# Modulation sums moved from the gate/up layer to the down layer, and a third buffer for raw gate/up weights

## The reference, cut to what matters

```python
def swiglu(u, w_gate_up, w_down):            # D_FF = 2816 = 22 x 128
    gate, up = jnp.split(u @ w_gate_up, 2, axis=-1)
    return (jax.nn.silu(gate) * up) @ w_down
...
    c_act = jax.nn.silu(c)                   # c: one row of 1024
    for layer in range(DEPTH_2):             # 2 layers, after the feed-forward
        mod = c_act @ ada_w[layer] + ada_b[layer]      # 1024 -> 3072
        shift, scale, gate = jnp.split(mod, 3, axis=-1)
        h = rms_norm(x, norm_w[layer]) * (1.0 + scale[:, None, :]) + shift[:, None, :]
```

## Time and profile before

| what | us |
|---|---|
| median of 3 runs | 2910.16 |
| lowest and highest of them | 2908.41, 2910.83 |
| the profiled execution | 2912.97 |
| its span | 2911.1 |
| PE busy | 2809.6 (97%) |
| DVE busy | 1868.6 (64%) |
| ACT busy | 1298.0 (45%) |
| POOL busy | 720.9 (25%) |

### The profile page before, as it was taken

The page is one execution under the profiler, slowest core; times in us unless marked ns, Lnnn a source line. Parts: engine busy times, 40 slices in busy tenths (PEclk is TensorE's granted clock), DMA queues, the critical chain, the costliest instruction groups (busy, mean ns, idle before and its releaser), DMA issues.

```text
span 2911.1 us, 37370 instructions
## 1 busy us (share of the span) xinstructions
PE 2809.6 (97%) x14198; PEld 2344.0 (81%) x14198; DVE 1868.6 (64%) x2554; ACT 1298.0 (45%) x2086; POOL 720.9 (25%) x921
## 2 busy tenths in 40 slices
PE   8999999999999999999999999899999899999998
PEld 7877787778888778888888778788888778888986
DVE  7564475764456788887334745789878745318974
ACT  5321347432454322223112345678767624417851
POOL 0000003300002666663000011466545200004520
PEclk9999999999999999999999999999999999999999
DMA  4111333232311344446311323100001331131032
GB/s 150 54 44 56 124 107 135 93 116 87 102 59 55 106 151 156 144 148 227 105 47 42 111 73 91 40 1 16 8 15 37 109 109 40 48 94 65 18 117 73
DMA packets 201521, 245.46 MB, mean 84 GB/s; under 512 B 11776, under 2 KB 152320, under 8 KB 199808
## 3 DMA queue, kind: packets, MB, share of 16 engines
q1 hardware_dynamic: 184320, 186.37, 20.0%
q0 software_dynamic: 9104, 28.32, 3.2%
q10 hardware_dynamic: 7920, 28.38, 2.9%
HBM read 192.11 MB, written 46.20 MB: 82 GB/s over the span
## 4 chain that ended last, share of the span: by engine, by line
PE 83%; DVE 8%; issue 2%; ACT 2%; POOL 2%; DMA 1%; ACTq 0%; DVEq 0%; SPq 0%; POOLq 0%
PE P L349 47%; PE P L286 5%; PE P L289 5%; PE P L291 5%; PE P L290 5%; PE P L2728 4%; PE P L318 2%; PE P L2742 2%; PE P L2741 1%; PE P L1116 1%; PE P L1590 1%; PE P L3334 1%; DVE U L1839 1%; POOL T L2990 1%; PE P L3328 1%
## 5 line engine op out<-in xcount | busy, mean ns | idle before, releaser
L273 DVE TENSOR_TENSOR wl<-wf,wh 128x1024 fp32r<-128x1024 f32 (+3 forms) x163 | 192.8, 1183 | 658.9 <-ACT wh L265 658.4
L265 ACT ACTIVATE wh<-wf 128x1024 fp32r<-128x1024 f32 (+3 forms) x163 | 167.0, 1025 | 766.7 <-PE P L349 705.5
L349 PE MATMUL P<-XH,wh 128*128 128x512 f32 (+1 forms) x1232 | 385.1, 394 | 6.2 <-DVE TMP L1393 2.5
L349 PE MATMUL P<-XL,wh 128*128 128x512 f32 (+1 forms) x1232 | 381.3, 391 | 0.0
L349 PE MATMUL P<-XH,wl 128*128 128x512 f32 (+1 forms) x1232 | 381.0, 391 | 0.0
L2990 POOL TENSOR_TENSOR T<-T,WST 128x512 f32<-128x512 f32 x256 | 260.9, 1040 | 219.8 <-DVE WST L2960 197.0
L349 PEld LDWEIGHTS P<-XH,wh 128*128 128x128 f32 (+1 forms) x1232 | 229.4, 187 | 61.4 <-issue 12.0
L349 PEld LDWEIGHTS P<-XH,wl 128*128 128x128 f32 (+1 forms) x1232 | 229.8, 187 | 51.1
L349 PEld LDWEIGHTS P<-XL,wh 128*128 128x128 f32 (+1 forms) x1232 | 229.8, 187 | 51.0
L289 PE MATMUL P<-FO,U 128*128 128x512 f32 x616 | 242.6, 394 | 8.3 <-DVE T L2103 6.6
L290 PE MATMUL P<-FO,U 128*128 128x512 f32 x616 | 240.1, 390 | 0.0
(11 more groups left out here) (478 smaller groups left out, 6257.1 us busy)
## 6 DMA issues: line engine op xcount, KB each, us to landing
AW<-ada_t POOLq DMA_DIRECT2D x96, 256.0 KB, 3.5
wf<-gu_units SPq DMA_DIRECT2D x88, 256.0 KB, 3.0
H<-scratch_h SPq DMA_DIRECT2D x32, 512.0 KB, 6.3
wf<-w_in SPq DMA_DIRECT2D x28, 512.0 KB, 3.8
scratch_h<-H SPq DMA_DIRECT2D x24, 512.0 KB, 5.7
scratch_g<-T ACTq DMA_DIRECT2D x22, 512.0 KB, 3.0
scratch_f<-T ACTq DMA_DIRECT2D x22, 512.0 KB, 3.2
wf<-odd_w_in SPq DMA_DIRECT2D x20, 512.0 KB, 4.0
```

The costliest lines, as they stand in the source:

```text
L265: e.activation(self.sb["wh"][i % 2][:, 0:m], self.sb["wf"][i % 2][:, 0:m], ACT.Copy).then_inc(*self.s.w_hi.up(i))
L273: e.tensor_tensor(l, f, h.bitcast(F32), ALU.subtract).then_inc(*self.s.w_lo.up(i))
L349: ins = e.matmul(self.P[slot][0:m, t:t1], w, x[:, k, t:t1], start=first and k == 0, stop=last and k == kb - 1)
```

## The change

All 48 columns of the modulation leave the gate/up layer. They are now loaded as whole rows of 1024 numbers (48 loads of 512 KB) and summed by one instruction each, three behind each of the first 16 tiles of the down layer, on DVE behind the low part of the block. The places for them are one new place in region A and two of the scratch tiles (`T[3]`, `T[1]`), which are free once the last pair is done. The load of `c` and its silu also move to the end of the gate/up layer; POOL's loads start there. The space of the old halves becomes a third raw place (`UR`), so the load of unit `u` waits for the low part of unit `u-3`, and unit 2's for the end of the layer before (`wo`, tile 7), whose input lies there until then.

```diff
     def raw(self, u):
-        return self.sb["wf"][(self.no["wo", 6] + u) % 2]
+        return (self.sb["wf"][self.no["wo", 7] % 2], self.sb["wf"][self.no["wo", 6] % 2], self.sb["UR"])[u % 3]
...
     def sp_unit(self, e, u):
-        e.wait_ge(*self.s.w_lo.to(("u", u - 2) if u > 1 else self.no["wo", 6 + u]))
-        e.dma_start(self.raw(u)[:, 0:512], self.dr["gu_units"][u]).then_inc(*self.s.u[u % 2].up(u))
+        if u == 2:
+            e.wait_ge(*self.s.mm.to(("wo", 7)))
+        else:
+            e.wait_ge(*self.s.w_lo.to(("u", u - 3) if u > 2 else self.no["wo", 7 - u]))
+        e.dma_start(self.raw(u)[:, 0:512], self.dr["gu_units"][u]).then_inc(*self.s.u[u % 3].up(u))
...
-    def dve_ada(self, e, h):
...
+    def pool_ada(self, e, n):
+        f = 128 * (n % 24)
+        if n > 2:
+            e.wait_ge(*self.s.dve.to(("ada", n - 3)))
+        e.dma_start(self.sb["AW"][n % 3], self.dr["ada_t"][n // 24][f:f + 128, :]).then_inc(*self.s.a[n % 3].up(n))
+
+    def dve_ada(self, e, n):
+        x, a = self.sb["AW"][n % 3], VECS["ada_b_2"][0] + n
+        e.wait_ge(*self.s.a[n % 3].to(n))
+        if n == 0:
+            e.wait_ge(*self.s.act.to("silu c"))
+        e.tensor_tensor_reduce(x, x, self.sb["AA"][:, :], 1.0, self.sb["vecs"][:, a:a + 1], ALU.mult, ALU.add,
+                               self.sb["MOD"][:, n:n + 1]).then_inc(*self.s.dve.up(("ada", n)))
+        if n % 8 == 7:
+            self.dve_ada_gain(e, n // 8)
...  sp_ffn
-        e.wait_ge(*s.w_lo.to(("u", UNITS - 2)))
+        e.wait_ge(*s.w_lo.to(("u", UNITS - 3)))
...
-            if b == 7:
-                e.wait_ge(*s.dve.to(("ada", 95)))
...  pool_ffn
-        for u in range(4):
+        for u in range(UNITS):
             self.pool_unit(e, u)
-        e.wait_ge(*self.s.mm.to(("wo", 7)))
+        e.wait_ge(*self.s.mm.to(self.unit_done(UNITS - 1)))
         e.dma_start(self.sb["AA"][:, :], self.dr["c_row"].partition_broadcast(128)).then_inc(*self.s.cr.up("in"))
         self.pool_ada(e, 0)
...
+        e.wait_ge(*self.s.dve.to(("ff", PAIRS - 1)))
+        for n in range(1, 48):
+            self.pool_ada(e, n)
...  act_ffn, behind the store of the last pair
+        e.wait_ge(*s.cr.to("in"))
+        e.activation(self.sb["AA"][:, :], self.sb["AA"][:, :], ACT.Silu).then_inc(*s.act.up("silu c"))
...  dve_ffn
-            for h in range(96):
-                if self.ada_unit(h) == u:
-                    self.dve_ada(e, h)
...  behind a tile of groups 0 and 1
                 if j < count:
                     self.dve_ffn_block(e, GROUPS[n + 1][0] + j)
+                for i in range(3):
+                    self.dve_ada(e, 24 * n + 3 * j + i)
```

More of the change, by code:

```diff
@@ L83 @@
             "act", "dve", "pool")
-    DMAS = ("w0", "w1", "vecs", "consts", "me", "m0", "m1", "dt", "a0", "a1", "ax", "xr", "rt", *(f"q{u}{n}" for u in range(2) for n in range(2)), "cr", "u0", "u1", "fs", "b0", "b1", "r0", "r1", "r2", "r3", "r4", "out",
+    DMAS = ("w0", "w1", "vecs", "consts", "me", "m0", "m1", "dt", "a0", "a1", "ax", "xr", "rt", *(f"q{u}{n}" for u in range(2) for n in range(2)), "cr", "u0", "u1", "u2", "a2", "fs", "b0", "b1", "r0", "r1", "r2", "r3", "r4", "out",
             *(f"f{n}{j}" for n in range(2) for j in range(8)), *(f"h{j}" for j in range(8)), *(f"g{j}" for j in range(8)), *(f"gl{j}" for j in range(8)))
@@ L97, in __init__ @@
         self.m = [m["m0"], m["m1"]]
-        self.a, self.ax, self.xr, self.rt = [m["a0"], m["a1"]], m["ax"], m["xr"], m["rt"]
+        self.a, self.ax, self.xr, self.rt = [m["a0"], m["a1"], m["a2"]], m["ax"], m["xr"], m["rt"]
         self.q, self.b, self.out = [[m[f"q{u}{n}"] for n in range(2)] for u in range(2)], [m["b0"], m["b1"]], m["out"]
         self.h = [m[f"h{j}"] for j in range(8)]
-        self.cr, self.fs, self.u = m["cr"], m["fs"], [m["u0"], m["u1"]]
+        self.cr, self.fs, self.u = m["cr"], m["fs"], [m["u0"], m["u1"], m["u2"]]
         self.f = [[m[f"f{n}{j}"] for j in range(8)] for n in range(2)]
@@ L1817, in pool_unit @@
         count = self.s.pool
-        e.wait_ge(*self.s.u[u % 2].to(u))
+        e.wait_ge(*self.s.u[u % 3].to(u))
         e.tensor_tensor(s1, a21, a22, ALU.add).then_inc(*count.up(("s1", u)))
@@ L1840, in dve_unit @@
                             ALU.subtract).then_inc(*self.s.w_lo.up(("u", u)))
[L1844 to L1854, removed]
-    def dve_ada(self, e, h):
[L1857 to L1861, removed]
-            e.wait_ge(*self.s.act.to("silu c"))
[L1863 to L1868, removed]
+    def pool_ada(self, e, n):
[7 more added lines that the diff above has]
+        if n == 0:
+            e.wait_ge(*self.s.act.to("silu c"))
+        e.tensor_tensor_reduce(x, x, self.sb["AA"][:, :], 1.0, self.sb["vecs"][:, a:a + 1], ALU.mult, ALU.add,
+                               self.sb["MOD"][:, n:n + 1]).then_inc(*self.s.dve.up(("ada", n)))
+        if n % 8 == 7:
+            self.dve_ada_gain(e, n // 8)
     def dve_ada_gain(self, e, i):
@@ L1875, in dve_ada_gain @@
         if part == 1:
-            e.wait_ge(*self.s.dve.to(("ada", 16 * i + 15)))
+            e.wait_ge(*self.s.dve.to(("ada", 8 * i + 7)))
             e.scalar_tensor_tensor(out=MOD, in0=MOD, scalar=1.0, in1=vecs[:, gain[0] + 8 * layer:gain[0] + 8 * layer + 8],
@@ L1954, in pool_ffn @@
     def pool_ffn(self, e):
-        for u in range(4):
+        for u in range(UNITS):
             self.pool_unit(e, u)
-        e.wait_ge(*self.s.mm.to(("wo", 7)))
+        e.wait_ge(*self.s.mm.to(self.unit_done(UNITS - 1)))
         e.dma_start(self.sb["AA"][:, :], self.dr["c_row"].partition_broadcast(128)).then_inc(*self.s.cr.up("in"))
         self.pool_ada(e, 0)
[L1960 to L1963, removed]
-            for h in range(96):
-                if self.ada_unit(h) + 3 == u:
-                    self.pool_ada(e, h + 2)
+        e.wait_ge(*self.s.dve.to(("ff", PAIRS - 1)))
+        for n in range(1, 48):
+            self.pool_ada(e, n)
     def pe_ffn(self, e):
@@ L2062, in act_ffn @@
                 e.activation(T[0][:, 0:512], self.gu_bank(m, 0), ACT.Copy).then_inc(*s.act.up(("p1", m)))
-            if u == 9:
-                e.wait_ge(*s.cr.to("in"))
-                e.activation(self.sb["AA"][:, :], self.sb["AA"][:, :], ACT.Silu).then_inc(*s.act.up("silu c"))
         for b in range(3, 7):
@@ L3718, in places @@
     sb["FX"] = put("FX", "X", 0, [128, 8, 2, S], F32R)
-    sb["AW"] = [put(f"AW{i}", "X", 28 * K + 2 * K * i, [128, 512], F32)[:, :] for i in range(2)]
-    sb["AA"] = put("AA", "X", 60 * K, [128, 1024], F32)
+    sb["UR"] = put("UR", "X", 28 * K, [128, 1024], F32)
+    sb["AW"] = [put("AW0", "A", 60 * K, [128, 1024], F32)[:, :], sb["T"][3], sb["T"][1]]
+    sb["AA"] = put("AA", "A", 56 * K, [128, 1024], F32)
     sb["ACC2"] = put("ACC2", "X", 60 * K, [128, 1024], F32)
```

## The result

The changed kernel takes 2917.19 us (median of 19 runs) against 2910.83 us of the kernel before (19 runs on the same chips): a ratio of 1.0019, 95% interval [1.0012, 1.0026]. I had forecast 2904.1 us, 0.2% faster; by the ratio it is about 5.5 us slower. A second set of runs of both kernels gave 1.001 [1.0002, 1.0019], about 3 us slower.

The account below looks back on a forecast made before the run. PE was taken to set the time. Gate/up -9.4, unit 2's load 0, down-layer DVE 0 and tile 2 +3.3 sum to -6.1 us; from the median 2910.16 that gives 2904.1 us, range 2899.7 to 2909.5.

Parts of the forecast that it names:

- the six stalls from the third pair on go: Gate/up layer: PE's six stalls from the third pair on vanish, part of the -9.4 us.
- 1.59 us for a stall of 1.64: Gate/up layer, stall at 1247.78: two modulation halves on DVE ahead of the drain, 1.59 us, explain PE's wait of 1.64 us.
- this stall goes: Gate/up start, stall at 948.77 (1.38 us): unit 4's raw load waits for unit 1 instead of unit 2, so it vanishes.
- Cost 0; if the sums drag, 1 us: Gate/up start: unit 2's load, some 6 us later, still arrives in time; 0 us, or 1 us if POOL's sums drag.
- the stall at 952.25: Gate/up start: this 0.42 us stall on the norm's chain, which moves with PE, stays.
- the term that I had forecast: Gate/up layer: stalls removed, -9.4 us, with bounds of -4.5 and -11.3 us.
- +3.3 us: Down layer, tile 2: stall from slab 2 delayed by POOL's loads and the last store, 2.85 + 2.55 - 2.1 us.
- rival 4: Down layer: slab 2 lands behind everything, +5.85 us, net -3.6 us, 2906.6 us; chance 0.10.
- 2.85 + 2.55: Down layer: slab 2's delay, 2.85 us from `c` and row 0, 2.55 us from rows 1 and 2 and the store.
- I take half: Down layer: half of the 5.1 us of rows 1 and 2 and the store goes ahead of slab 2, 2.55 us.
- 1.30 estimated: Down layer, DVE: each modulation sum over 1024 numbers takes 1.30 us, fits idle time and costs PE 0.
- rival 3: Down layer: DVE runs at the pace of the modulation loads, deciding from 7.9 us a load; 2927 us; chance 0.07.

Follow-up runs that it names:

- e1: The changed kernel without its third raw place (two as before), modulation sums still in the down layer; ratio 0.9995 to the kernel before.
- e9: The kernel before with only the first two of POOL's 96 modulation loads, all DVE sums kept on other data; ratio 0.9984 to the kernel before.
- e12: e6 with POOL holding unit 4's sums until DVE has done the last four differences of the input forms; ratio 0.9968 to the kernel before.
- e6: The changed kernel with down slabs 2 and 3 ahead of the blocks and the third raw place used only from unit 4; ratio 0.9971 to before.
- e3: The kernel before with the load of down slab 2 held until PE ends tile 1; ratio 1.0023 to the kernel before.
- e4: The changed kernel with POOL's loads of modulation rows 1 and 2 held until ACT has split slab 2; ratio 0.9997 to the kernel before.
- e11: The kernel before with blocks 10 to 14 held until PE ends down tile 0, slab 2 behind them; ratio 1.003 to the kernel before.
- e2: The changed kernel with down slabs 2 and 3 issued ahead of the eight FXF blocks; ratio 0.9977 to the kernel before.

## Why the prediction was wrong

**Later pairs: the outcome right, the reason only in part.** I said that the six stalls from the third pair on go. They did, in every kernel without the modulation in that layer. But I credited both edits, and e1 shows that the third place has no part in it. And I read their cause off the two halves that stand ahead of a drain, 1.59 us for a stall of 1.64. e9 keeps these halves and the long stalls are gone. The larger part was in the waits, by the chain above POOL's for DVE, a line of 92.1 us in the earlier trace rows that I had passed over as costing nothing by itself.

**First pairs: the step failed.** I wrote of the stall at 948.77 that "this stall goes", and of unit 2's later load "Cost 0; if the sums drag, 1 us". The sums dragged: 4.8 us for unit 2, where the four took 2.7 us for unit 2 before, because the later load put them under DVE's differences and splits, and they slowed DVE in turn. Unit 2 was 0.9 us late, then units 3 and 4; the norm's chain began at 946.22 instead of 944.24; the stall grew to 2.2 us, with a new one of 0.3 us in front, and the clock fell behind it for 3.4 us. Against my sum that is 1.7 us not won, 1.8 us lost and 1.7 us for the clock, less 0.7 us for the stall at 952.25, which went under in the longer one: 4.5 us, against the 4.0 us by which the stretch misses the forecast and by which it is longer than e12's, which has none of these. e12's stretch is 9.4 us below before, the term that I had forecast. In e6 and e12 the stall at 948.77 did go, by the mechanism I gave: the idea held for unit 4 and failed by the place chosen for unit 2.

**Unpriced: the clock.** My sum put nothing for what PE loses by the clock after a stall. In these two layers the clock fell at the stalls of 3.8 to 6.6 us at tile 2 (the change twice, e1, e3, e4, e11) and behind the one of 2.2 us at 951 us (the change twice, e2, e4), and not at the single ones of 1.5 to 1.8 us in the kernel before and in e1. At tile 2 it fell between 3.6 us before PE went on (e11) and 1.4 us after (e4). It stayed at half for 3.4 or 6.8 us, part of that within the stall, and cost 1.6 to 3.0 us beyond the stall each time. No run has a stall between 2.2 and 3.8 us, or varies what goes ahead of one.

**Tile 2: the right mechanism, the wrong size.** The term was +3.3 us, bounds 0.75 to 5.85. The stall measured 5.9 and 6.6 us, my rival 4 and a little more, and with the clock the layer lost 9.0 and 9.4 us. The slab came 8.0 us later, where I had 2.85 + 2.55 = 5.4 us. `c` and row 0 took 4.3 us of it, not 2.85 (e4 and the landing times). And the step "I take half" failed: the store and rows 1 and 2 landed at 1374.0, 1374.8 and 1376.2, all ahead of slab 2 at 1377.5, and took the other 3.7 us. It is the order of landing of rival 4. Slab 2 stood in SP's queue behind 4 MB of blocks. Its first bytes moved 18.1 us after the layer's first matmul, in the kernel before 11.7 us after it, so 6.4 of the 8.0 us had passed before it began; the landings of the block loads before it had reached 17.4 us from their issue, where they had reached 9.4. With slab 2 issued first (e2) it landed 3.7 us after its issue, though `c` and row 0 were issued 0.3 and 1.0 us behind it. So its place in the queue made the most of the delay; what its short pieces add isn't shown. The Trainium skill (DMA: Bandwidth & Descriptors, Issuing engines are not separate DMA queues) says that all DMAs interleave on the same engines; the traces agree: POOL's and ACT's transfers landed between SP's blocks.

**Down layer, DVE: right.** 1.28 us a sum against 1.30 estimated, and rival 3 did not occur: the rows landed after 5.0 us in the median, under the 7.9 us from which it would decide (those in the burst after 9.5 to 10.4 us), and e2's down layer is as short as before.

**The sum again,** with measured terms: -5.4 + 9.2 (mean of the two) = +3.8 us, a ratio of 1.0013. The two sets of runs gave 1.0019 and 1.0010, whose intervals hold it.

## What to carry to other kernels

When work is moved off a busy stage, list what its loads will meet at the new place: here 1 MB issued at the same moment as a burst, and 1 MB more at its end, delayed the one transfer with a small margin, and putting the needed slabs at the head of the burst cured it. A stall of PE can cost more than its length: here the clock fell at all ten of 2.2 us and more, and at none of the single ones of up to 1.8 us. And an engine that stands in its list behind a wait for another, as POOL did, can be the cause of a stall whose name in the profile is that of a third.

## What the runs showed of the hardware

- A late slab with no added traffic (e3) brought the clock down as much as the change did: 0.52 of full speed in the 7 us from 1383, the first 2.2 of them still within the 6.5 us stall.
- POOL and DVE slowed each other where they ran at once on operands in SBUF: a sum of 128 columns on POOL took 0.9 to 2.5 us instead of 0.46 us, one of 512 columns on DVE 0.95 us instead of 0.68 us.
- The broadcast load of `c`, 512 KB, landed after 4.5 us at the start of the gate/up layer, where only two loads of POOL's stood beside it, and after 8.4 us in the burst.
